# Two chains of small steps on one TensorE: filler products between the two steps of a round, or behind both

## The chip, the cores and the metric

The kernel runs on one core of a Trainium2 chip, in one launch. The metric is the device time of that launch in microseconds (us), the median of several runs. A profiled execution of the same program gives the trace; its span is a little shorter than its time, since the start and the end lie outside it.

The engines are named as in the profile: PE is TensorE's matmul, PEld its weight load, DVE is VectorE, ACT ScalarE, POOL GpSimd, SP SyncE, which issues the DMAs. Each runs its own list of instructions in order, and they wait for each other by semaphores.

## The reference

Sequence 1024, width 1024, batch 1, float32. A first block of two layers (convolution and LRU mixer, mLSTM mixer, two SwiGLUs) is followed by one hybrid layer, and only a stage of that layer is touched:

```python
h = rmsnorm(x, norm_gain)
proj = h @ w_in
(...) = jnp.split(proj, IN_OFFSETS, axis=-1)
ys = (
    gated_deltanet(...),           # chunks of 64, a triangular inverse in each
    spatial_gating(...),
    rwkv7_time_mix(...),
    native_sparse_attention(...),  # compressed, selected and window attention
)
gates = jnp.split(jax.nn.sigmoid(merge), N_MIXERS, axis=-1)
mixed = gates[0] * (ys[0] @ w_branch[0])
for i in range(1, N_MIXERS):
    mixed = mixed + gates[i] * (ys[i] @ w_branch[i])
return x + mixed @ w_out
```

`merge` is the last 4096 columns of `proj`. Nothing in the four mixers needs them, they are only needed at the merge.

## The kernel before, in words

Every float32 product is made of three matmuls on split operands: `xhalf` (high and low part) by `whi`, and `xhalf` by `wlo` (L476). A weight block `wraw` of 128x1024 comes by DMA (L315), ScalarE rounds it to `whi` (L325), GpSimd takes `wlo` (L333), and VectorE, ScalarE and SyncE take away the results.

**The stage of the scans** is the part from 2802 to 3612 us of the profile. Three kinds of work stand in it:

- **Stream A**: the gated deltanet, then the preparations of the sparse attention. Written as a Python generator for each engine; between two `yield`s stands one *step*. A step on PE is a handful of matmuls, and the next step of the stream needs what VectorE and ScalarE made of them.
- **Stream B**: the spatial gating of the two halves, three empty steps (`wait_steps(RWKV_LATER)`), then the RWKV recurrence in chunks.
- **Gates**: the 512 products of `h` with the merge columns (2 halves x 32 tiles x 8 products). A *gate step* is one such product on PE. On the other engines the same step count moves on the rest of it: the split of the next weight block (L325 on ACT, L333 on POOL), and after every eighth product the scaling (L2775 on DVE), the tanh (L2792 on ACT) and the store `g_keep` and the next `wraw` load on SP (L2815, L315). They depend on neither stream and are there to fill PE.

**What sets the order** is `weave_beside`: it takes one step of A, then one of B, and so on, and counts them both, so that A's steps have the odd numbers and B's the even ones. An A step and the B step after it are called a round here; there are some 167 rounds in the stage. Behind *each* step it takes 1 + `MORE_GATES`[number] gate steps. The same call with the same numbers orders all five engines, so that their lists agree. Below, A313 is step 313, of stream A, and B314 the one after it.

`MORE_GATES` holds most extra products behind A steps: 12 behind A1, 5 behind A47, A111 and A115, 7 behind A251, 6 behind A313; and 7 and 8 behind B226 and B228. SyncE has a table of its own, `LOADS_AHEAD`, which differs only in steps 1 and 4.

Where the steps stand in the code: A1 is the matmuls L2941 of `rows`, B2 those of `sg` (L2941 too, in the spatial gating), A3 is L2875. In B, L3592 to L3610 are the two kinds of step of the RWKV chunks late in the stage, and L3719 and L3725 are what VectorE makes of them. In A, L3989 belongs to the compressed attention and needs what L4039 to L4042 make on VectorE.

The attention after the scans uses the same function for its own streams.

Of the kernel before, what the change touches and what calls it, by code (L numbers as in the profile page):

```python
# [870 lines left out]
def wait_steps(n):  # L871
    for _ in range(n):
        yield
# [1105 lines left out]
def rounds(*streams):  # L1979

    live = list(streams)
    while live:
        for s in list(live):
            if next(s, StopIteration) is StopIteration:
                live.remove(s)
        yield
# [1431 lines left out]
def spatial_tensor(pe, K, Q, H, B, j):  # L3418
    n, mm = ("sg", j), pe.e.matmul
    spread_tensor(pe, K, Q, (n, "mean"), H.heads, B.V[:, j, :], (n, "in"), halves=2)  # L3420
    yield from wait_steps(3)
    sums_tensor(pe, K, Q, H, (n, "rs"), B.sq[:, j, :])
    yield from wait_steps(3)
    back_tensor(pe, K, Q, (n, "rs"), B.sq[:, j, :], 2)
    yield from wait_steps(3)
    turn_tensor(pe, K, Q, (n, "vt"), B.V[:, j, :], (n, "normed"), halves=2)
    yield from wait_steps(2)
    pe.wait_ge(*K.at("causal sg"))
    for q in range(2):
        b = take(pe, K, Q, n, "mix", q)  # L3430
        pe.wait_ge(*K.at((n, "vt"), "rows"))
        bias = H.sg_b[0:4, :].unsqueeze(1).to_broadcast([4, 4, 128])
        mm(K.ps[:, b, :], H.pair[0:4, j, :], bias, start=True, stop=False, skip_group_check=True)
        for s in range(2):
            p = part(s, 64)
            for i in range(4):
                d = mm(K.ps[p, b, part(i)], B.VT[:, j, 4 * q + i, p], H.sg_w[:, 2 * j + s, :], start=False, stop=True, skip_group_check=True)
        d.then_inc(*K.T((n, "mix", q)))
    yield
    yield  # L3440


def spatial_vector(ve, K, H, B, j):
    n, V = ("sg", j), K.V
    x, rs, u = B.V[:, j, :], B.rs[:, j, :], B.U[:, j, :]
    yield
    for h in range(2):
        ve.wait_ge(*K.at((n, "mean"), "mm", h))
        ve.own().scalar_tensor_tensor(out=x[:, HALVES[h]], in0=K.bank((n, "mean"), h), scalar=-1.0 / 64, in1=x[:, HALVES[h]], op0=MUL, op1=ADD).then_inc(*V((n, "centred"), ("free", ((n, "mean"), h))))
    yield from wait_steps(3)  # L3450
    sums_vector(ve, K, (n, "rs"), B.rows[j], 1e-5)
    yield
    back_vector(ve, K, (n, "rs"), B.rows[j], B.sq[:, j, :])
    yield from wait_steps(3)
    ve.wait_ge(*K.at((n, "rs"), "rs"))
    ve.own().tensor_tensor(x, x, rs, MUL).then_inc(*V())
    ve.own().tensor_scalar(x, x, K.vec("sg_ln_gain", j), K.vec("sg_ln_bias", j), MUL, ADD).then_inc(*V((n, "normed")))
    yield
    ve.own().tensor_tensor(u, u, B.Z[:, j, :], MUL).then_inc(*V())
    yield from wait_steps(3)  # L3460
    for q in range(2):
        ve.wait_ge(*K.at(n, "mix", q))
        ve.own().tensor_tensor(u[:, HALVES[q]], u[:, HALVES[q]], K.bank(n, "mix", q), MUL).then_inc(*V((n, "y"), ("free", (n, "mix", q))))
    yield


def spatial_scalar(se, K, H, B, j):
    n = ("sg", j)
    yield from wait_steps(2)
    square_scalar(se, K, (n, "rs"), B.V[:, j, :], B.sq[:, j, :], (n, "centred"))  # L3470
    yield from wait_steps(5)
    back_scalar(se, K, (n, "rs"), B.rs[:, j, :], 2)
    yield from wait_steps(3)
    turn_scalar(se, K, (n, "vt"), B.VT[:, j, :, :], halves=2)
    yield from wait_steps(3)


def spatial_gpsimd(ge, K, H, B, j):
    yield from wait_steps(4)
    sums_gpsimd(ge, K, (("sg", j), "rs"), B.rows[j])  # L3480
    yield from wait_steps(SPATIAL_STEPS - 4)
# [8 lines left out]
def spatials(stream):  # L3490

    return rounds(stream(0), in_turn(wait_steps(1), stream(1)))
# [806 lines left out]
LOADS_AHEAD = {**MORE_GATES, 1: 0, 4: 12}  # L4299


def weave_beside(gates, *streams, more={}):

    live, steps = list(streams), 0
    while live:
        for s in list(live):
            if next(s, StopIteration) is StopIteration:
                live.remove(s)
            steps += 1
            for _ in range(1 + more.get(steps, 0)):  # L4310
                next(gates, None)


RWKV_LATER = 3
# [26 lines left out]
def in_turn(*streams):  # L4341
    for s in streams:
        yield from s


def scans_tensor(pe, K, R):
    H, g, s, w = R.H, R.gdn, R.sg, R.rw
    QA, QB = K.QA, K.QB
    pe.wait_ge(*K.at("hybrid constants"))
    gates = gates_tensor(pe, K, H.N)  # L4350
    weave_beside(gates, in_turn(gdn_tensor(pe, K, QA, H, g), nsa_tensor(pe, K, QA, H, R.nsa)),
                 in_turn(spatials(lambda j: spatial_tensor(pe, K, QB, H, s, j)), wait_steps(RWKV_LATER), rwkv_tensor(pe, K, QB, H, w)), more=MORE_GATES)
    pe.reach("scanned")

    def first():
        given_up(pe, K, QA, QB)
        chosen_tensor(pe, K, R.nsa)

    attend_streams(gates, staggered(lambda kind, h: attend_tensor(pe, K, R.nsa, kind, h, K.QC)), wait_steps(ATTEND_STEPS), first=first)


def scans_vector(ve, K, R):
    H, g, s, w = R.H, R.gdn, R.sg, R.rw
    gates = gates_vector(ve, K, H.N, R)
    weave_beside(gates, in_turn(gdn_vector(ve, K, H, g), nsa_vector(ve, K, H, R.nsa)),
                 in_turn(spatials(lambda j: spatial_vector(ve, K, H, s, j)), wait_steps(RWKV_LATER), rwkv_vector(ve, K, H, w)), more=MORE_GATES)
    ve.reach("scanned")

    def first():
        ve.after(K, "scanned")  # L4370
        chosen_vector(ve, K, R.nsa)

    attend_streams(gates, staggered(lambda kind, h: attend_vector(ve, K, H, R.nsa, kind, h)), wait_steps(ATTEND_STEPS), first=first)
    ve.mine.mark(("attended",))


def scans_scalar(se, K, R):
    H, g, s, w = R.H, R.gdn, R.sg, R.rw
    gates = gates_scalar(se, K, H.N, R)
    weave_beside(gates, in_turn(gdn_scalar(se, K, H, g), nsa_scalar(se, K, H, R.nsa)),  # L4380
                 in_turn(spatials(lambda j: spatial_scalar(se, K, H, s, j)), wait_steps(RWKV_LATER), rwkv_scalar(se, K, H, w)), more=MORE_GATES)
    se.reach("scanned")
    attend_streams(gates, staggered(lambda kind, h: attend_scalar(se, K, R.nsa, kind, h)),
                   in_turn(at_steps(*(lambda i=i: results_back_scalar(se, K, R, i) for i in range(2))), wait_steps(ATTEND_STEPS - 16)), first=lambda: se.after(K, "scanned"))


def scans_gpsimd(ge, K, R):
    H, g, s, w = R.H, R.gdn, R.sg, R.rw
    gates = gates_gpsimd(ge, K)
    weave_beside(gates, in_turn(gdn_gpsimd(ge, K, H, g), wait_steps(NSA_STEPS)),  # L4390
                 in_turn(spatials(lambda j: spatial_gpsimd(ge, K, H, s, j)), wait_steps(RWKV_LATER), rwkv_gpsimd(ge, K, H, w)), more=MORE_GATES)
    ge.reach("scanned")
    attend_streams(gates, staggered(lambda kind, h: wait_steps(ATTEND_STEPS)),
                   in_turn(at_steps(*(lambda i=i: results_back_gpsimd(ge, K, R, i) for i in range(2))), wait_steps(ATTEND_STEPS - 16)), first=lambda: ge.after(K, "scanned"))


def scans_sync(sy, K, R, chunk0):
    g, s, w, B = R.gdn, R.sg, R.rw, R.nsa

    def rwkv_first():  # L4400
        yield from wait_steps(12)
        for j in range(2):
            sy.wait_ge(*K.at((("sg", j), "vt"), "turned"))
        rwkv_load(sy, K, w, 0, 0)

    sy.after(K, "hy projected")
    sy.projected(K)
    gates = gates_sync(sy, K, R.H.N, R, chunk0)
    weave_beside(gates, in_turn(gdn_sync(sy, K, g, lambda: nsa_load(sy, K, B)), nsa_sync(sy, K, B)),
                 in_turn(rounds(spatials(lambda j: spatial_sync(sy, K, s, j)), rwkv_first()), wait_steps(RWKV_LATER), rwkv_sync(sy, K, w)), more=LOADS_AHEAD)  # L4410

    def first():
        sy.wait_ge(*K.at("y kept", 1))
        sy.after(K, "scanned")
        attend_load(sy, K, B)
        for i in range(2):
            results_back_sync(sy, K, R, i)

    attend_streams(gates, staggered(lambda kind, h: wait_steps(ATTEND_STEPS)),
                   in_turn(wait_steps(6), at_steps(*(lambda i=i: results_back_sync(sy, K, R, i) for i in range(2, 4))), wait_steps(ATTEND_STEPS - 22)), first=first, lead=8)  # L4420
# [742 lines left out]
```

## Time and profile before

| | us |
|---|---|
| median of 3 runs | 4012.09 |
| lowest, highest | 4011.49, 4012.41 |
| profiled execution: its time | 4012.28 |
| its span | 4010.5 |
| PE busy in the span | 3772.6 |
| DVE, ACT, POOL busy | 2630.1, 1343.8, 1193.1 |
| the scans (2802 to 3612): length, PE busy | 810.0, 766.7 |
| DVE, ACT, POOL busy in them | 413.0, 226.8, 185.6 |

The profiled execution is within 0.2 us of the median, so that sums made on its trace can be laid on the median. A busy PE is not a PE at full speed: PEclk is the share of the full TensorE clock that was granted in a stretch, 1.00 being 2.4 GHz and 0.50 1.2 GHz.

### The profile page before, as it was taken

How to read it: one execution, taken by the hardware profiler on the slowest of the kernel's cores; microseconds unless marked ns; L12 is line 12 of the kernel's file. 1: busy time of each engine (PE TensorE's matmuls, PEld its weight loads, DVE VectorE, ACT ScalarE, POOL GpSimd, SP SyncE). 2: the span in 40 equal slices, each digit the busy share in tenths (PEclk: the TensorE clock that was granted, in tenths of full speed). 3: DMA queues.
4: the chain of work that ended last, by engine and by line, in shares of the span. 5: the costliest groups of instructions: out<-in, count | busy, mean ns of one | idle time of the engine just before them, and what ended most of it. 6: DMA issues, size and time to landing. Idle time of an engine off the chain costs nothing.

```text
span 4010.5 us, 51700 instructions
## 1 busy us (share of the span) xinstructions
PE 3772.6 (94%) x20718; PEld 2957.9 (74%) x20718; DVE 2630.1 (66%) x2926; ACT 1343.8 (34%) x1756; POOL 1193.1 (30%) x578
## 2 busy tenths in 40 slices
PE   8999899999889999999999998999999989998998
PEld 7567788877666666778887776887777767776777
DVE  6964887789874554378788988741455454547783
ACT  5243432234333333243223434211333232324522
POOL 2012144444313333214444441222222212222064
PEclk9999999999989999999999998999999989999999
DMA  3002233345320010222324532323312222323063
GB/s 114 21 21 89 100 101 107 108 154 183 120 80 32 32 37 22 90 105 89 108 93 166 181 121 96 109 91 107 125 59 69 82 72 72 118 89 95 34 209 142
DMA packets 131768, 385.57 MB, mean 96 GB/s; under 512 B 13564, under 2 KB 14208, under 8 KB 126280
## 3 DMA queue, kind: packets, MB, share of 16 engines
q1 hardware_dynamic: 131528, 382.27, 27.5%
q8 instruction: 163, 2.67, 0.3%
q14 instruction: 77, 0.63, 0.0%
HBM read 281.00 MB, written 101.22 MB: 95 GB/s over the span
## 4 chain that ended last, share of the span: by engine, by line
PE 71%; DVE 22%; ACT 4%; issue 1%; POOL 1%; DMA 1%; DVEq 0%; SPq 0%; ACTq 0%; POOLq 0%
PE ps L380 22%; PE ps L1453 21%; PE ps L476 9%; PE ps L4476 2%; PE ps L907 2%; PE ps L2250 1%; PE ps L2971 1%; DVE top L1626 1%; DVE acc L1722 1%; PE ps L2242 1%; DVE xop L1626 1%; PE ps L3064 1%; DVE x L661 1%; PE ps L2988 1%; DVE t L641 1%
## 5 line engine op out<-in xcount | busy, mean ns | idle before, releaser
L333 POOL TENSOR_TENSOR wlo<-wraw,whi 128x1024 fp32r<-128x1024 f32 x181 | 447.8, 2474 | 1712.1 <-ACT whi L325 1703.7
L1453 PE MATMUL ps<-xop,whi 128*128 128x512 f32 x1984 | 617.7, 393 | 14.7 <-DVE acc L1747 9.8
L325 ACT ACTIVATE whi<-wraw 128x1024 fp32r<-128x1024 f32 x185 | 196.1, 1060 | 887.6 <-PE ps L380 605.4
L1453 PE MATMUL ps<-top,whi 128*128 128x512 f32 x1488 | 470.7, 398 | 19.7 <-DVE acc L1716 15.9
L1453 PEld LDWEIGHTS ps<-xop,whi 128*128 128x128 f32 x1984 | 373.0, 188 | 99.7 <-DVE acc L1747 12.3
L1453 PE MATMUL ps<-xop,wlo 128*128 128x512 f32 x992 | 388.2, 391 | 0.0
L476 PE MATMUL ps<-xhalf,whi 128*128 128x512 f32 x1024 | 369.7, 443 | 0.2 <-POOL wlo L333 0.2
L1453 PEld LDWEIGHTS ps<-top,whi 128*128 128x128 f32 x1488 | 282.3, 190 | 88.3 <-DVE acc L1716 19.1
L1851 POOL TENSOR_TENSOR wlo<-wsum,whi 128x1024 fp32r<-128x1024 f32 (+2 forms) x102 | 228.9, 2244 | 363.5 <-ACT whi L1478 363.0
L380 PE MATMUL ps<-xhi,whi 128*128 128x512 f32 x868 | 306.7, 435 | 18.8 <-DVE xlo L681 6.7
L1453 PE MATMUL ps<-top,wlo 128*128 128x512 f32 x744 | 294.7, 396 | 0.0
L380 PE MATMUL ps<-xhalf,whi 128*128 128x512 f32 x1012 | 273.9, 393 | 11.0 <-DVE xhalf L681 8.6
L380 PE MATMUL ps<-xlo,whi 128*128 128x512 f32 x868 | 273.0, 396 | 0.0
L380 PE MATMUL ps<-xhi,wlo 128*128 128x512 f32 x868 | 271.7, 395 | 0.0
L1851 POOL TENSOR_TENSOR wlo<-wraw,whi 128x1024 fp32r<-128x1024 f32 (+2 forms) x80 | 182.6, 2283 | 245.5 <-ACT whi L1478 243.6
L380 PEld LDWEIGHTS ps<-xhalf,whi 128*128 128x128 f32 x1012 | 191.0, 189 | 53.5 <-DVE xhalf L681 11.2
L476 PEld LDWEIGHTS ps<-xhalf,whi 128*128 128x128 f32 x1024 | 178.0, 198 | 53.4 <-issue 23.7
L1453 PEld LDWEIGHTS ps<-xop,wlo 128*128 128x128 f32 x992 | 186.7, 188 | 41.0
L380 PEld LDWEIGHTS ps<-xhi,whi 128*128 128x128 f32 x868 | 161.0, 193 | 74.5 <-issue 27.4
L476 PE MATMUL ps<-xhalf,wlo 128*128 128x512 f32 x512 | 209.1, 408 | 0.0
L1478 ACT ACTIVATE whi<-wsum 128x1024 fp32r<-128x1024 f32 (+2 forms) x108 | 101.9, 943 | 299.9 <-PE ps L1453 126.7
L380 PEld LDWEIGHTS ps<-xlo,whi 128*128 128x128 f32 x868 | 165.9, 191 | 36.8
(641 smaller groups left out, 7091.4 us busy)
## 6 DMA issues: line engine op xcount, KB each, us to landing
wraw<-in_w_dram SPq DMA_DIRECT2D x185, 512.0 KB, 3.6
h_keep<-h SPq DMA_DIRECT2D x154, 256.0 KB, 4.5
wraw<-in_s_dram SPq DMA_DIRECT2D x48, 512.0 KB, 4.1
f<-h_keep SPq DMA_DIRECT2D x24, 768.0 KB, 5.4
wmore<-in_s_dram SPq DMA_DIRECT2D x32, 512.0 KB, 4.0
x_keep<-x SPq DMA_DIRECT2D x16, 1024.0 KB, 3.8
g_keep<-gates SPq DMA_DIRECT2D x64, 256.0 KB, 2.4
gb<-g_keep SPq DMA_DIRECT2D x32, 512.0 KB, 4.1
```

The costliest lines, as they stand in the source:

```text
L325: se.own().activation(K.hi(c), K.raw[:, c % NRAW, :], ACT.Copy).then_inc(*K.S(("hi", c)))
L333: ge.own().tensor_tensor(K.lo(c), K.raw[:, c % NRAW, :], K.hi(c).bitcast(F32), SUB).then_inc(*K.G(("lo", c)))
L380: done = pe.e.matmul(into[:, h, :], wt, x[h], start=(first and j == 0), stop=(last and j == 2), skip_group_check=True)
L476: done = mm(K.ps[:, b, :], wt, x, start=(i == 0 and j == 0), stop=(i == n - 1 and j == 2), skip_group_check=True)
L641: ve.own().tensor_tensor(acc, acc, sq, ADD).then_inc(*K.V((n, "add", i), (n, "add")))
L661: ve.own().tensor_tensor(X[:, i, :], X[:, i, :], Y.out[:, i, :], ADD).then_inc(*K.V((n, "x", i)))
L907: d = mm(K.ps[:, banks[h], :], M.diag[:, (BY_PE.index(j) * P_TAPS + k) % NDIAG, :], M.Yc[:, j, 512 * h + k:512 * h + k + 512], start=(k == ...
L1453: d = pe.e.matmul(out[:, s, :], w[:, o], x[:, i, :], start=(j < 3 and i == 0 and t == 0), stop=(i == k - 1 and t == 2), skip_group_check=True)
L1478: se.own().activation(F.whi(c), F.source(b, j), ACT.Copy).then_inc(*K.S((n, "whi", c)))
L1626: ve.own().tensor_tensor(F.olo[j][:, :k, :], source[:, :k, :], F.ohi[j][:, :k, :].bitcast(F32), SUB).then_inc(*K.V((F.name, "op", g, j)))
L1851: seat.own().tensor_tensor(F.wlo(c), F.source(b, j), F.whi(c).bitcast(F32), SUB).then_inc(*signal((F.name, "wlo", c)))
L4476: done = mm(into, w, x, start=(i == 0 and j == 0), stop=(i == 7 and j == 2), skip_group_check=True)
```

## The change

`weave_beside` gets an argument `behind`. Without it, gate steps follow each step as before. With `behind=-1`, the gate steps that are due are only counted, and are taken behind the step of the last stream that is still live, that is behind B's. So a round was A, its gates, B, its gates; it is A, B, and the gates of both. When one stream has ended, the other is the last one, and gates follow each of its steps. All five calls in the scans get `behind=-1`; the attention's call doesn't.

```diff
-def weave_beside(gates, *streams, more={}):
-
-    live, steps = list(streams), 0
+def weave_beside(gates, *streams, more={}, behind=None):
+
+    live, steps, due = list(streams), 0, 0
     while live:
         for s in list(live):
             if next(s, StopIteration) is StopIteration:
                 live.remove(s)
             steps += 1
-            for _ in range(1 + more.get(steps, 0)):
-                next(gates, None)
+            due += 1 + more.get(steps, 0)
+            if behind is None or not live or s is live[behind]:
+                for _ in range(due):
+                    next(gates, None)
+                due = 0
...
-                 in_turn(spatials(lambda j: spatial_tensor(pe, K, QB, H, s, j)), wait_steps(RWKV_LATER), rwkv_tensor(pe, K, QB, H, w)), more=MORE_GATES)
+                 in_turn(spatials(lambda j: spatial_tensor(pe, K, QB, H, s, j)), wait_steps(RWKV_LATER), rwkv_tensor(pe, K, QB, H, w)), more=MORE_GATES, behind=-1)
```

PE, start of the stage. `rows` are A1's operands, `sg` B2's, `xhalf` by `whi` and `wlo` is a gate product (a pair of rows), and L2875 is A3; 13 such pairs are taken away and put back in the two gaps:

```order
 L2941 MATMUL ps<-rows,c_175 128x512 x2
-L476 MATMUL ps<-xhalf,whi 128x512 x2
-L476 MATMUL ps<-xhalf,wlo 128x512
...
 L2941 MATMUL ps<-sg,c_175 128x512 x2
 L476 MATMUL ps<-xhalf,whi 128x512 x2
 L476 MATMUL ps<-xhalf,wlo 128x512
+L476 MATMUL ps<-xhalf,whi 128x512 x2
+L476 MATMUL ps<-xhalf,wlo 128x512
...
 L2875 MATMUL ps<-c_175,g 128x2 x8
```

The 13 products that stood between A1 and B2 stand behind B2 now, 14 in a row before A3.

PE, late in the stage, around A313 (the first L3989) and B314 (L3606, L3610); again 7 pairs go and come in the gaps:

```order
 L3989 MATMUL ps<-const,n 128x128 x4
-L476 MATMUL ps<-xhalf,whi 128x512 x2
-L476 MATMUL ps<-xhalf,wlo 128x512
...
 L3606 MATMUL ps<-r 128x128
 L3610 MATMUL ps<-r 64x128 x2
 L476 MATMUL ps<-xhalf,whi 128x512 x2
 L476 MATMUL ps<-xhalf,wlo 128x512
+L476 MATMUL ps<-xhalf,whi 128x512 x2
+L476 MATMUL ps<-xhalf,wlo 128x512
...
 L3989 MATMUL ps<-const,n 128x128 x4
```

The seven products between A313 and B314 are behind B314. VectorE's rows at this place do not change up to L3719.

ACT, around B42. L3761 and L2915 make the operands of B42 on PE (L2875 of `r`), L2792 is the tanh of a finished gate tile, L325 a weight split:

```order
 L325 ACTIVATE whi<-wraw 128x1024
-L2792 ACTIVATE gates<-ps 128x512
 L3761 ACT_TABLE_LOAD
 L3761 ACTIVATE r<-ps,vec 128x512 x2
 L2915 ACTIVATE r<-r 128x512
-L325 ACTIVATE whi<-wraw 128x1024
+L2792 ACTIVATE gates<-ps 128x512
 L3768 ACT_TABLE_LOAD
```

The tanh of the gate tile now stands behind stream B's three operations instead of ahead of them. PE has the same rows in both kernels, 9217 when equal neighbours are taken together, in another order.

## Rows read from the trace of the kernel before

**Rows 1.** Page, part 1: busy time, share of span and instructions by engine.

```profile
PE 3772.6 (94%) x20718; PEld 2957.9 (74%) x20718; DVE 2630.1 (66%) x2926; ACT 1343.8 (34%) x1756; POOL 1193.1 (30%) x578
```

**Rows 2.** Windows: length, busy of PE, PEld, DVE, ACT, POOL; PEclk, DMA share, GB/s.

```profile
2802.00:3612.00 810.00, 766.74 (x7674) 594.65 (x7675) 412.96 (x692) 226.76 (x340) 185.57 (x79) 0.93 0.26 87
...
3240.00:3305.00 65.00, 52.78 (x263) 38.94 (x264) 37.91 (x62) 21.87 (x36) 8.58 (x4) 0.76 0.18 61
...
3095.74:3100.00 4.26, 4.26 (x15) 3.52 (x17) 2.19 (x4) 0.00 (x0) 0.00 (x0) 0.50 0.01 3
...
2903.00:2910.00 7.00, 6.71 (x85) 5.47 (x86) 3.67 (x10) 0.24 (x1) 0.00 (x0) 0.76 0.23 90
```

**Rows 3.** Waits of PE, 2802 to 3612: total us, times, longest.

```profile
PE ps L3064 <- DVE r L3679: 9.2, 3, 4.1
...
PE ps L2875 <- ACT r L2915: 3.6, 2, 2.1
```

**Rows 4.** Timeline of PE, stage start: start, us, line, count, idle before.

```profile
2802.19 2.08 PE L2941 MATMUL ps<-rows,c 4*128 4x512 f32 x4 [3.84 <-POOL wlo L333]
2804.20 1.22 PE L476 MATMUL ps<-xhalf,whi 128*128 128x512 f32 x2
...
2808.20 0.84 PE L476 MATMUL ps<-xhalf,whi 128*128 128x512 f32 x2
...
2815.27 1.88 PE L2941 MATMUL ps<-sg,c 128*128 128x512 f32 x4
...
2817.68 1.51 PE L2875 MATMUL ps<-c,g 128*128 128x2 f32 x13
```

**Rows 5.** Tile `sg`, 2800 to 2819: its loads, and their time to landing.

```profile
L2860 SPq DMA_DIRECT2D sg<-p_keep x6: 432/452/707, 2805.7 to 2808.6; - x6
...
DMA to landing us min/median/max: 5.7/7.6/9.1
```

**Rows 6.** Timeline of PE around A313 and B314.

```profile
3551.15 0.66 PE L3989 MATMUL ps<-const,n 128*128 128x128 f32 x4 [0.93 <-DVE n L4042]
...
3556.67 0.49 PE L3606 MATMUL ps<-r 128*128 128x128 f32 x2
...
3558.26 0.60 PE L3989 MATMUL ps<-const,n 128*128 128x128 f32 x4
```

**Rows 7.** Timeline of DVE at the same place.

```profile
3546.37 0.59 DVE L3725 SCALAR_TENSOR_TENSOR r<-r,ps 64x64 f32<-64x64 f32 x2 [2.34 <-PE ps L3606]
3547.07 1.22 DVE L4039 TENSOR_REDUCE n<-n 128x16 f32<-128x1024 f32 x1
...
3556.32 0.29 DVE L3719 SCALAR_TENSOR_TENSOR r<-ps,r 128x128 f32<-128x128 f32 x1
```

**Rows 8.** Timeline of ACT ahead of B42.

```profile
2895.92 1.06 ACT L325 ACTIVATE whi<-wraw 128x1024 fp32r<-128x1024 f32 x1 [6.91 <-PE ps L476]
2899.17 0.60 ACT L2792 ACTIVATE gates<-ps 128x512 f32<-128x512 f32 x1 [2.19 <-DVE ps L2775]
2899.87 1.28 ACT L3761 ACT_TABLE_LOAD   x1
...
2902.61 0.63 ACT L2915 ACTIVATE r<-r 128x512 f32<-128x512 f32 x1
```

**Rows 9.** Timeline of PE after B124's wait.

```profile
3095.74 2.08 PE L3064 MATMUL ps<-r 64*128 64x128 f32 x8 [4.09 <-DVE r L3679]
```

**Rows 10.** Timeline of PE, switches between products and small steps.

```profile
3180.73 0.73 PE L476 MATMUL ps<-xhalf,whi 128*128 128x512 f32 x2
...
3182.32 1.15 PE L2971 MATMUL ps<-inv 64*64 64x64 f32 x32
...
3188.20 0.73 PE L476 MATMUL ps<-xhalf,whi 128*128 128x512 f32 x2
...
3189.09 0.27 PE L2988 MATMUL ps<-inv 64*64 64x64 f32 x1
```

**Rows 11.** Weight loads (PEld) by line, 2802 to 3612.

```profile
L2988 PEld LDWEIGHTS ps<-inv 64*64 64x64 f32 x1280 | 44.3, 144 | 15.8 <-issue 12.8 <-DVE ps L2775 1.4 <-DVE r L3644 0.4
```

More of the change, by code:

```diff
@@ L4365, in scans_vector @@
     weave_beside(gates, in_turn(gdn_vector(ve, K, H, g), nsa_vector(ve, K, H, R.nsa)),
-                 in_turn(spatials(lambda j: spatial_vector(ve, K, H, s, j)), wait_steps(RWKV_LATER), rwkv_vector(ve, K, H, w)), more=MORE_GATES)
+                 in_turn(spatials(lambda j: spatial_vector(ve, K, H, s, j)), wait_steps(RWKV_LATER), rwkv_vector(ve, K, H, w)), more=MORE_GATES, behind=-1)
     ve.reach("scanned")
@@ L4380, in scans_scalar @@
     weave_beside(gates, in_turn(gdn_scalar(se, K, H, g), nsa_scalar(se, K, H, R.nsa)),
-                 in_turn(spatials(lambda j: spatial_scalar(se, K, H, s, j)), wait_steps(RWKV_LATER), rwkv_scalar(se, K, H, w)), more=MORE_GATES)
+                 in_turn(spatials(lambda j: spatial_scalar(se, K, H, s, j)), wait_steps(RWKV_LATER), rwkv_scalar(se, K, H, w)), more=MORE_GATES, behind=-1)
     se.reach("scanned")
@@ L4390, in scans_gpsimd @@
     weave_beside(gates, in_turn(gdn_gpsimd(ge, K, H, g), wait_steps(NSA_STEPS)),
-                 in_turn(spatials(lambda j: spatial_gpsimd(ge, K, H, s, j)), wait_steps(RWKV_LATER), rwkv_gpsimd(ge, K, H, w)), more=MORE_GATES)
+                 in_turn(spatials(lambda j: spatial_gpsimd(ge, K, H, s, j)), wait_steps(RWKV_LATER), rwkv_gpsimd(ge, K, H, w)), more=MORE_GATES, behind=-1)
     ge.reach("scanned")
@@ L4409, in scans_sync @@
     weave_beside(gates, in_turn(gdn_sync(sy, K, g, lambda: nsa_load(sy, K, B)), nsa_sync(sy, K, B)),
-                 in_turn(rounds(spatials(lambda j: spatial_sync(sy, K, s, j)), rwkv_first()), wait_steps(RWKV_LATER), rwkv_sync(sy, K, w)), more=LOADS_AHEAD)
+                 in_turn(rounds(spatials(lambda j: spatial_sync(sy, K, s, j)), rwkv_first()), wait_steps(RWKV_LATER), rwkv_sync(sy, K, w)), more=LOADS_AHEAD, behind=-1)
     def first():
```

## The prediction, made before the changed kernel ran

> **What bounds the kernel now.** I read the page first: PE is busy for 94% of the span, the next engine, DVE, for 66% [rows 1]. Then the windows, for the stage of the scans alone, since all that moves stands in it. PE is busy for 766.7 of 810 us there, DVE for 413.0; 43.3 us of PE are idle, and the mean granted clock is 0.93 [rows 2]. The clock stands at full or half, so 0.93 means that about (1 - 0.93) x 810 / 0.5 = 113 us of the stage ran at 1.2 GHz. The stage is bound by PE's list of work in most places, and by the chains of the two streams in some: from 3240 to 3305 PE is busy for only 52.8 of 65 us and its clock is 0.76 [rows 2]. The waits of PE name those places: the longest sum, 9.2 us in three waits, is of B steps for DVE, another 3.6 us in two for an ACT row of stream B [rows 3]. No wait for gate operands is of weight. The work itself stays as it is, so there are four things to price: places where the gate products were cover for a transfer or another engine and no longer are, places where stream B gets its operands sooner, the cost of switching PE between products and small steps, and the clock.
>
> **The rule for cover.** Between A(k) and A(k+1) PE still has the gates and the B step, and between B(k) and B(k+1) the gates and the A step. What a step can hide before its own stream's next step is nearly unchanged; only the extra products behind an A step now lie one step later for B. A stream B step loses if its operands become ready late in those products. So I compared, for each B step, when its operands were ready with when PE came to it. At the large blocks behind A47, A111, A115, A179, A251 and A303 the operands had been ready for longer than the moved products take, or the B step is empty. Two places are left, A1 and A313.
>
> **Start of the stage: +9.** A1 runs at 2802.19, thirteen products begin at 2804.20, and B2 begins at 2815.27, A3 at 2817.68 [rows 4]. B2 needs `sg`, six loads of 512 KB issued from 2805.7 to 2808.6, which land in up to 9.1 us [rows 5]. That puts the first load, which B2 waits for, between 2811.4 and 2814.8; the trace's event for it is at 2813.9, so that PE had 1.35 us to spare. With the change B2 stands directly behind A1, so PE has nothing to do from 2804.2 to 2813.9, 9.7 us. Then come B2, 2815.27 to the next product at 2816.59 = 1.32 us, and fourteen products. Ten products from 2808.20 to B2 at 2815.27 are 7.07 us, 0.71 each with the switch at their end, 0.69 without. A3 then begins at 2813.9 + 1.3 + 14 x 0.69 = 2824.9, 7.2 us late. That is the low end of this edit. The high end adds the clock. At 2804.20 the engine came from 3.84 us of idle time, and its first three products took (2808.20 - 2804.20) / 3 = 1.33 us each; after B124's wait of 4.09 us a row of eight matmuls lasts 2.08 us, and the window behind it has a granted clock of 0.50 [rows 2, 4, 9]. If B2 and three products run so, 1.3 + 3 x 0.64 = 3.2 us come on top: +10.4. I take +9, nearer to the high end, since both such waits of the trace were followed by the half clock. A later wait of stream B could swallow some of it; this puts the low end at +5.
>
> The Trainium skill, page "TensorE: Matmul & The Clock Gate", section "HAM oscillation — how this bites in real kernels", speaks against the change here: idle gaps between bursts of matmuls send the array back to 1.2 GHz, and the next burst pays. Rows 9 agree with it, with 2.08 us at clock 0.50. By it both new gaps would be at their high ends; without it both at the low ones.
>
> **A313 and B314: +5.** A313 begins at 3551.15 and gives way at 3551.56 to seven products; B314 begins at 3556.67 and A315 at 3558.26 [rows 6]. B314 waits for L3719, and on DVE eight operations of the attention (L4039 to L4042, twice) stand from 3547.07 ahead of it; L3719 runs from 3556.32 to 3556.61 [rows 7]. So seven products, 3551.56 to 3556.6, hid DVE work. The order of DVE does not change there, so B314 stays at 3556.67, or 0.7 us sooner at best, as L3725 at 3546.37 may come one product earlier. PE idles for 5.1 us, and then has B314 (0.78 us, to the next product) and eight products: 3556.67 + 0.78 + 8 x 0.69 = 3562.97 for A315, against 3558.26: +4.7. Low end with the 0.7 us: +4.0; high end with B314 and four products at half clock, + 0.4 + 4 x 0.6: +7.5. I take +5.
>
> **B42: -2.** B42 waited for ACT's L2915, for 2.1 of the 3.6 us in rows 3. L2915 at 2902.61 stands behind L3761's table load at 2899.87, and this behind a gate's tanh at 2899.17, for which ACT had been idle for 2.19 us [rows 8]. The tanh moves behind L2915. L3761 can then begin after L325, from 2897.0 if its operand is there, which it must be by 2899.87. L2915 ends up to 2.9 us sooner; PE's wait of 2.1 us can go in full but no more. So between 0 and -2.1, and another -1.7 if the half-clock stretch behind this wait goes too: from 2903 to 2910 the clock is 0.76 [rows 2], and (1 - 0.76) x 7 = 1.7. I take -2.
>
> **Switches: -9.** Two products in a row between 64-row steps take 3182.32 - 3180.73 = 1.59 us, one alone 3189.09 - 3188.20 = 0.89 us, while one inside a run takes 0.70 [rows 10]. The difference of 0.19 is lost before the 64x64 weight load; the loads of L2988 alone sat idle for 12.8 us with "issue" as their only reason [rows 11]. The change merges the two places of products in a round into one, so it saves one such switch, if PE is not waiting for operands anyway. Of the rounds, 119 have matmuls in both steps, and in 24 of these PE waits at B. Where both steps are 64-row ones (some 18 rounds) I count 0.3 us, since the switch into the products costs some 0.1 as well: 5.4. In the 77 others, with 128-row steps on one side, a product takes 0.79 or less before the step, and I count 0.05: 3.6. Together -9. The ends: nothing but the 64-row rounds at 0.19, -4; and 0.19 in all 95, -18.
>
> The same page, section "Back-to-back issue gap", would give less: it has loads and matmuls pipelined, with spacing set by both, so that the order of unlike ones should not matter. Rows 10 show a gap that it does not tell of. By it this term is 0, and the sum +12.
>
> **Everything else: 0.** Gate work of ACT, DVE, POOL and SP moves behind B's rows by one step. That makes B's rows earlier and the gates' tiles free later by about 0.7 us; the weight split has blocks in hand, and no wait of rows 3 names it. In the stretches bound by chains, as 3240 to 3305, the chain is the same and the products only change sides. I take 0, between -2 and +4. SP's `g_keep` stores and weight loads also move behind B's loads, which are few.
>
> **The sum.** 9 + 5 - 2 - 9 + 0 = +3. On the profiled execution's 4012.28 this is 4015.3, on the median, 0.19 lower, 4015.1. Low ends together: 5 + 4 - 3.8 - 18 - 2 = -15; high ends: 10.4 + 7.5 + 0 - 4 + 4 = +18.
>
> **The rivals.**
> *Slower: the clock (4027).* One mechanism: PE's half-clock stretches follow idle time, and grouping makes idle time longer in one piece and products denser in another. Both gaps at their high ends, the switches worth only 4, and up to six further half-clock stretches at 1.7 us each, as after B42's wait: 10.4 + 7.5 - 2 - 4 + 10.2 = +22 at most, and +15 with two of them. It decides once the waits of a round fall together in the chain-bound stretches. For it: 113 us already run at half clock. Against: the total of idle time hardly changes apart from the two gaps.
> *Slower: cover lost one product at a time (4025).* PE comes to some 28 B steps within 0.1 us of their operands. If each moved forward by a product and found nothing, 28 x 0.69 = 19 us would be exposed, which with the +3 of the sum is +22; with half of them it is +12.7. Against: those operands come from the B step before, which moves forward as well. It decides only where B's operands come from A's DVE work, as at A313.
> *Faster: switches (4002).* Gaps at their low ends, 5 + 4, B42 -3.8, switches -15: -10. For it: "issue" stands behind a great part of PEld's idle time. Against: much of that is hidden behind the matmul before.
> *The change does nothing (4012).* If B2's operand were there at 2804, or DVE's block were reordered. Rows 5 and 7 exclude both.
>
> **How the numbers follow.** The forecast, two new gaps paid mostly by fewer switches: 0.58. Clock: 0.14. Lost cover: 0.13. Switches win: 0.13. Nothing: 0.02. A measurement tells 0.2%, 8 us, from no change. The forecast's own range is 4006 to 4023, so 0.05 of its 0.58 is beyond +8. Faster by over 8 us: 0.11 (most of its rival). Slower by over 8: 0.05 + 0.14 + 0.11 = 0.30. Within: 0.59. The range with 8 in 10 is 4003 to 4027.
>
> **What would show it.** On PE's timeline: idle time of 9 to 10 us behind A1, a `sg` step at half clock, and A3 some 9 us late; at A313 an idle stretch of 4 to 5 us that ends at L3719. L2915 ahead of L2792 on ACT and no wait at B42. Idle time of PEld by "issue" lower by about 9 us in the stage. PE's idle time in the scans up from 43 to about 56 us, while PE's busy time is up by the clock or down by the switches. Wrong would be: `sg` landing before A1 ends, a wait for L476's operands in the long runs, or new waits of B steps outside the two places.

## The result, and the profile after

The changed kernel takes 4035.6 us (median of 4 runs, 4034.1 to 4047.7) beside 4012.25 for the kernel before (median of 4, 4011.5 to 4021.0): 1.0052 times, 95% interval 1.0037 to 1.0068, or 15 to 27 us more. That is outside the predicted range of 4003 to 4027.

The profiled execution took 4034.1 us, span 4032.3. Inside the scans, from A1's first matmul to the end of the last step of stream B, it was 814.0 us beside 795.0 before, +18.9. The other 2.9 us of the two spans lie in stretches whose instructions are the same in both kernels, 1.5 of them ahead of A1.

Windows of the changed kernel, the scans from A1 to B334, then the first 4.0 us from B2 on and 3.6 us from B314 on; columns as in [rows 2]:

```profile
2803.68:3617.65 813.97, 743.44 (x7616) 588.54 (x7617) 414.74 (x686) 222.85 (x335) 179.98 (x77) 0.93 0.25 83
...
2816.90:2820.90 4.00, 3.97 (x6) 1.87 (x7) 0.00 (x0) 0.00 (x0) 0.00 (x0) 0.54 0.50 204
...
3571.40:3575.00 3.60, 3.57 (x11) 2.62 (x12) 1.95 (x4) 0.88 (x2) 0.00 (x0) 0.51 0.02 5
```

The same stretch of the kernel before:

```profile
2802.19:3597.22 795.03, 751.96 (x7616) 582.57 (x7617) 408.94 (x686) 222.84 (x335) 180.73 (x77) 0.93 0.25 86
```

PE is busy for 8.5 us *less* and idle for 70.5 us instead of 43.1. So PE's own work did become cheaper, and the loss is 27.5 us of new idle time. Not all of the 8.5 us belongs to the order, though. The kernel in which all engines but PE have the changed order was profiled twice (see the experiments). The two windows of its scans differ by 7.9 us of PE's busy time:

```profile
2805.14:3594.67 789.53, 748.93 (x7616) 581.03 (x7617) 407.85 (x686) 222.86 (x335) 179.88 (x77) 0.94 0.26 86
...
2801.73:3597.76 796.03, 756.80 (x7616) 587.12 (x7617) 408.80 (x686) 222.96 (x335) 179.13 (x77) 0.93 0.26 85
```

The first has 92.0 us of PE's busy time at half clock, the second 108.5. A matmul takes about twice as long at half clock (a product 1.28 us instead of 0.69, below), so busy time less half of its half-clock part is PE's work as if at full clock. In the scans that is 702.6 to 703.9 us in the ten traces in which PE's order is that of before or differs in one or two rounds, and 696.3 to 696.7 us in the four with all of its rounds, or all but two, joined; the three kernels with a part of the rounds joined lie between. So the order is worth 6.7 us of work, and the other 1.8 of the 8.5 are half-clock time that differs between the two traces (97.9 and 94.3 us).

The waits of PE, to be read beside [rows 3]; first two more of the kernel before:

```profile
PE ps L2941 <- DVE r L3669: 5.4, 4, 2.6
...
PE ps L3559 <- ACT r L2932: 3.0, 1, 3.0
```

and then those of the changed kernel:

```profile
PE ps L2941 <- DMA sg<-p_keep: 11.2, 1, 11.2
PE ps L3064 <- DVE r L3679: 8.9, 3, 4.1
PE ps L2941 <- DVE r L3669: 8.4, 4, 3.3
PE ps L3606 <- DVE r L3719: 5.5, 1, 5.5
PE ps L3559 <- ACT r L2932: 4.3, 2, 3.7
...
PE ps L2875 <- ACT r L2915: 2.7, 3, 2.1
...
PE ps L2988 <- DVE inv L3026: 2.2, 1, 2.2
```

The first and the fourth row are new and are the two places of the prediction, 16.7 us together. The rest, 10.8 us of new idle time, is spread over small waits of both streams: L3669's is up by 3.0 us, L2932's by 1.3, and L3026's, 2.2 us, is new. 5.9 of the 10.8 us lie in steps 189 to 229, from 3247 to 3369 us of the trace before, the stretch that the prediction called bound by chains.

The start of the stage on PE's timeline, for [rows 4]:

```profile
2803.68 2.08 PE L2941 MATMUL ps<-rows,c 4*128 4x512 f32 x4 [3.86 <-POOL wlo L333]
...
2816.93 3.78 PE L2941 MATMUL ps<-sg,c 128*128 128x512 f32 x4 [11.17 <-DMA sg<-p_keep]
2819.72 1.44 PE L476 MATMUL ps<-xhalf,whi 128*128 128x512 f32 x2
...
2821.24 0.62 PE L476 MATMUL ps<-xhalf,whi 128*128 128x512 f32 x2
...
2830.11 1.84 PE L2875 MATMUL ps<-c,g 128*128 128x2 f32 x16
```

From A1 to A3 are 26.43 us, 15.49 before: +10.9. B2 took 2.79 us to the next product instead of 1.32, at a granted clock of 0.54, and the first product 1.52 instead of 0.69. In return the three slow products behind A1 [rows 4] are gone: between A1 and A3 PE is busy at half clock for 5.7 us, 6.5 before. So here the slow work has only moved, and the +10.9 is the wait of 11.2 us. A313 and B314, for [rows 6]:

```profile
3565.24 0.66 PE L3989 MATMUL ps<-const,n 128*128 128x128 f32 x4 [0.23 <-DVE n L4042]
...
3571.43 0.79 PE L3606 MATMUL ps<-r 128*128 128x128 f32 x2 [5.54 <-DVE r L3719]
...
3572.78 1.22 PE L476 MATMUL ps<-xhalf,whi 128*128 128x512 f32 x2
...
3579.38 0.60 PE L3989 MATMUL ps<-const,n 128*128 128x128 f32 x4
```

From A313 to A315 are 14.14 us, 7.11 before: +7.0. The wait is 5.5 us of it, and B314 and the products behind it cost some 1.7 us more than at full clock. VectorE's rows are the ones of [rows 7], in the same order. On ACT, the table load for B42 stands ahead of the tanh, for [rows 8]:

```profile
2908.51 1.28 ACT L3761 ACT_TABLE_LOAD   x1
2909.81 1.41 ACT L3761 ACTIVATE r<-ps,vec 128x512 f32<-128x512 f32 x2
2911.31 0.63 ACT L2915 ACTIVATE r<-r 128x512 f32<-128x512 f32 x1
2912.05 0.60 ACT L2792 ACTIVATE gates<-ps 128x512 f32<-128x512 f32 x1
```

The weight loads have less idle time by "issue": those of L2988, for [rows 11], have half of it left, those of the products 13.9 of 23.2 us. First the kernel before, then the changed one:

```profile
L476 PEld LDWEIGHTS ps<-xhalf,whi 128*128 128x128 f32 x926 | 161.5, 199 | 50.3 <-issue 23.2 <-ACT gates L2792 0.2 <-POOL wlo L333 0.2
...
L476 PEld LDWEIGHTS ps<-xhalf,whi 128*128 128x128 f32 x928 | 173.1, 200 | 48.0 <-issue 13.9
L2988 PEld LDWEIGHTS ps<-inv 64*64 64x64 f32 x1280 | 43.3, 141 | 13.2 <-issue 6.4 <-DVE inv L3026 3.0 <-DVE ps L2775 2.2
```

These two rows alone are down by 15.7 us, where the prediction had looked for 9 in the whole stage, and PE's work fell by 6.7: most of a load's idle time had been hidden behind the matmul before it.

### The profile page after: what moved, and what is told of

Same layout as the page of the kernel before. It is cut to its first block, busy times and chain, and to the rows that moved or that the text cites. A ratio compares the mean times of both kernels' runs of the same rounds, so it can differ in the third digit from the quotient of the medians.

```text
span 4032.3 us, 51693 instructions
## 1 busy us (share of the span) xinstructions
PE 3766.4 (93%) x20718; PEld 2964.3 (74%) x20718; DVE 2639.7 (65%) x2926; ACT 1343.9 (33%) x1756; POOL 1195.5 (30%) x578
## 3 DMA queue, kind: packets, MB, share of 16 engines
q1 hardware_dynamic: 131528, 382.27, 27.5%
## 4 chain that ended last, share of the span: by engine, by line
PE 68%; DVE 24%; ACT 4%; issue 2%; POOL 1%; DMA 1%; DVEq 0%; SPq 0%; ACTq 0%; POOLq 0%
PE ps L380 22%; PE ps L1453 21%; PE ps L476 8%; PE ps L4479 2%; PE ps L907 2%; PE ps L2250 1%; DVE top L1626 1%; DVE acc L1722 1%; PE ps L2242 1%; DVE xop L1626 1%; PE ps L2971 1%; DVE x L661 1%; PE ps L3064 1%; PE ps L2988 1%; DVE t L641 1%
## 5 line engine op out<-in xcount | busy, mean ns | idle before, releaser
L325 ACT ACTIVATE whi<-wraw 128x1024 fp32r<-128x1024 f32 x185 | 196.1, 1060 | 933.2 <-PE ps L380 607.8
L1453 PE MATMUL ps<-top,whi 128*128 128x512 f32 x1488 | 471.6, 398 | 19.4 <-DVE acc L1716 16.0
L1453 PEld LDWEIGHTS ps<-xop,whi 128*128 128x128 f32 x1984 | 373.4, 189 | 99.4 <-DVE acc L1747 11.7
L476 PE MATMUL ps<-xhalf,whi 128*128 128x512 f32 x1024 | 358.3, 432 | 0.3 <-POOL wlo L333 0.3
L380 PE MATMUL ps<-xhalf,whi 128*128 128x512 f32 x1012 | 275.0, 394 | 10.4 <-DVE xhalf L681 7.9
L380 PEld LDWEIGHTS ps<-xhalf,whi 128*128 128x128 f32 x1012 | 191.7, 190 | 52.4 <-DVE xhalf L681 9.8
L476 PEld LDWEIGHTS ps<-xhalf,whi 128*128 128x128 f32 x1024 | 189.2, 199 | 51.0 <-issue 14.5
```

The lines of the kernel that those rows point to most:

```text
L325: se.own().activation(K.hi(c), K.raw[:, c % NRAW, :], ACT.Copy).then_inc(*K.S(("hi", c)))
L380: done = pe.e.matmul(into[:, h, :], wt, x[h], start=(first and j == 0), stop=(last and j == 2), skip_group_check=True)
L476: done = mm(K.ps[:, b, :], wt, x, start=(i == 0 and j == 0), stop=(i == n - 1 and j == 2), skip_group_check=True)
L1453: d = pe.e.matmul(out[:, s, :], w[:, o], x[:, i, :], start=(j < 3 and i == 0 and t == 0), stop=(i == k - 1 and t == 2), skip_group_check=True)
```

## A way to read two traces of reordered work

PE's matmuls other than the products (19182 of them) have the same order in both kernels. So the n-th of them in one trace is the n-th in the other, and the difference of their starts, less the one at A1, is how far the changed kernel has fallen behind at that step. Read at A steps it is +10.9 at A3, 9.9 at A41, 7.2 at A43, 5.7 at A47, 3.2 at A85, 6.2 at A91 to A121, 11.5 at A131, 9.5 at A141, 10.4 at A155 to A195, 7.0 at A209, 10.5 at A227, 9.7 to A255, 11.8 at A257, 12.6 at A313, 19.6 at A315 and 19.4 at A329. Two steps of +10.9 and +7.0 stand out. Between them it wanders from 2.1 (A81) to 13.3 (A295) and comes back to within 1.7 us of where it began. Whether the wandering means anything was a question for the chip.

A part of it comes from the trace of before, which is one execution too: in the nine other traces with PE's order as before but for a round or two, the distance to it falls by 3.1 us from A131 to A147, because that one trace has 13.7 us at half clock from A131 to A155 where they have 3.4.

## The experiments

Theory 1: two waits that lost their cover make up the loss. Theory 2: it is spread over many small waits and half-clock stretches. In the kernels that join rounds by number, `weave_beside` got one more condition, and `joined(step)` says after which steps the gate products may wait:

```diff
-            if behind is None or not live or s is live[behind]:
+            if behind is None or not live or s is live[behind] or not joined(steps):
```

Differences are to the kernel before, by the ratio of the runs and its interval, times 4014 us; "in the scans" is the difference between the traces in the length from A1 to the end of B334. Three of the kernels below ran only once and are read only at the place in question: the half cover, and rounds 41 and 39 alone.

**Only the first round joined:** `return step == 1`.

> Only the first round is joined (B2 directly behind A1, the 14 gate products behind B2); all other steps keep their order of before. Theory 1 (two waits that lost their cover make up nearly all of the loss, 10.9 us at A3 and 7.0 us at A315): +10 to +11 us on the kernel before, 4022 to 4023, with PE idle for some 11 us ahead of B2 and about 4 us at half clock behind it, and no other difference of over 1 us. Theory 2 (the loss is the sum of many small waits and of half-clock stretches that fall elsewhere; the place itself is partly taken back later by waits of stream B that it swallows): +3 to +7.

Measured: +0.37% (0.24 to 0.50), +15 us (10 to 20). In the scans +12.8, of which +12.0 at A3. Its timeline of PE:

```profile
2809.37 2.08 PE L2941 MATMUL ps<-rows,c 4*128 4x512 f32 x4 [3.82 <-POOL wlo L333]
2822.55 3.78 PE L2941 MATMUL ps<-sg,c 128*128 128x512 f32 x4 [11.10 <-DMA sg<-p_keep]
2836.85 0.39 PE L2875 MATMUL ps<-c,g 128*128 128x2 f32 x3
```

The wait and the half-clock B2 are there with this round alone, and none of it is given back later. The 12.0 us at A3 are 1 us above what theory 1 had expected, the +15 of the runs more, with +10 to +11 just inside their interval.

**Only the round of A313 and B314 joined:** `return step == 313`.

> Only the round of A313 and B314 is joined. Theory 1: +6 to +7 us on the kernel before, 4018 to 4019, PE idle for 5 us ahead of B314 and at half clock behind. Theory 2: +2 to +4, the rest of the 7 us seen in the changed kernel having come from work that was late already.

Measured: +0.25% (0.15 to 0.36), +10 us (6 to 14). In its trace A313 to A315 takes 14.76 us instead of 7.11, +7.7:

```profile
3549.75 0.66 PE L3989 MATMUL ps<-const,n 128*128 128x128 f32 x4 [0.94 <-DVE n L4042]
...
3555.24 0.80 PE L3606 MATMUL ps<-r 128*128 128x128 f32 x2 [4.83 <-DVE r L3719]
...
3560.60 1.06 PE L476 MATMUL ps<-xhalf,whi 128*128 128x512 f32 x2
...
3564.51 0.60 PE L3989 MATMUL ps<-const,n 128*128 128x128 f32 x4
```

The wait is 4.8 us, and the fourth product at 3560.60 still lasts 1.06 us a pair where one at full clock lasts 0.62: four products at half clock, 1.28 us each, against one to two in the changed kernel. So theory 1 has its second place, 0.7 us dearer in the trace than its upper end of 7.

**Both places left as before, all other rounds joined:** `return step not in (1, 313)`.

> The changed kernel with A1 and A313 followed by their own gate products again, as before; all other rounds are joined. Theory 1: the 17.9 us of the two places go, 4034.1 - 17.9 = 4016, that is +2 to +5 on the kernel before, since the new small waits (about 11 us more idle time of PE outside the two places) stand against the 9 us of PE time saved by fewer switches. Theory 2: the gain is under 12 us and the time stays at or over 4022.

Measured: -0.09% (-0.20 to +0.02), -4 us (-8 to +1). In the scans +3.1. With the two places taken out the loss is gone, and 15 + 10 us of the two alone are, within their intervals, the 21 us of the whole. Theory 2 is excluded, and theory 1 holds, though the time lies a little under its range of +2 to +5. But the window shows that the rest is not the gain of 11 us that the prediction had added up for it:

```profile
2803.97:3602.06 798.09, 743.57 (x7616) 588.97 (x7617) 413.45 (x686) 222.73 (x335) 179.45 (x77) 0.93 0.25 85
```

PE is busy for 8.4 us less than before (6.6 of them work, the rest less half-clock time) and idle for 54.5 us, 11.5 more.

**Half of the cover at each place,** with the order of before:

```diff
-MORE_GATES = {1: 12, 18: 3, ... 303: 2, 313: 6}
+MORE_GATES = {1: 6, 2: 6, 18: 3, ... 303: 2, 313: 3, 314: 3}
-LOADS_AHEAD = {**MORE_GATES, 1: 0, 4: 12}
+LOADS_AHEAD = {**MORE_GATES, 1: 0, 2: 0, 4: 12}
```

> The order of before, but the extra products of the two places are shared: 7 products behind A1 and 7 behind B2 (13 and 1 before), 4 behind A313 and 4 behind B314 (7 and 1 before). It is read at the two places on the trace. If the loss is the missing cover alone, six products fewer ahead of B2 make PE wait for 2 to 4 us and A3 comes 3 to 4 us later against A1 than before; at A315 1.5 to 2.5 us later, with an idle stretch of about 2 us. If half-clock work after the wait is a part of the price at any length of wait, 1.5 to 2.5 us come on top at each; if it needs the long wait, the granted clock stays at 1.00 behind both waits.

Measured: A3 5.9 us later, A315 2.1 us later. PE's timeline:

```profile
2816.70 3.64 PE L2941 MATMUL ps<-sg,c 128*128 128x512 f32 x4 [4.08 <-DMA sg<-p_keep]
2819.50 1.31 PE L476 MATMUL ps<-xhalf,whi 128*128 128x512 f32 x2
...
3564.66 0.49 PE L3606 MATMUL ps<-r 128*128 128x128 f32 x2 [2.12 <-DVE r L3719]
...
3565.45 0.73 PE L476 MATMUL ps<-xhalf,whi 128*128 128x512 f32 x2
```

Six products fewer, 4.1 us, made 4.1 us of wait, and the matmuls after it ran at half clock, 1.8 us more. Three fewer at the other place, 2.1 us, made 2.1 us of wait and no half-clock work: B314 and the product behind it last what they last before. So half-clock work came on top behind the wait of 4.1 us and not behind the one of 2.1. The cost of missing cover is its length, plus what half-clock work follows.

**Only the stretches where the distance fell / stayed / rose.** `joined` is true for steps 41 to 81, 131 to 147 and 203 to 213; for 91 to 121, 157 to 187 and 229 to 255; and for 123 to 129, 149 to 153, 195 to 201, 217 to 221, 225 to 227, 257 and 295.

> Only the rounds of steps 41 to 81, 131 to 147 and 203 to 213 are joined: the stretches in which the changed kernel came nearer to the one before (at A steps, by 7.8, 2.1 and 6.0 us). If those gains belong to the places, -10 to -16 us on the kernel before. If they are a matter of where the half-clock stretches happen to fall, -2 to -6, with the fall at 203 to 213, where no wait changed, missing.

> Only the rounds of steps 91 to 121, 157 to 187 and 229 to 255 are joined, 46 rounds in stretches bound by PE with 64x64 steps of stream A beside 128-row steps of B. In the changed kernel A's steps kept their distance to the kernel before within 0.3 us through each. Theory: one switch less saves nothing there, -1 to +1. The rival, the prediction's term of switches: 0.05 to 0.19 us a round, -2.5 to -9.

> Only the rounds of steps 123 to 129, 149 to 153, 195 to 201, 217 to 221, 225 to 227, 257 and 295 are joined: the stretches bound by chains in which the changed kernel fell back, by some 17 us in all. If the new waits are due to the joined order at the place, +8 to +17; if they follow from half-clock stretches that fall elsewhere, 0 to +5.

Measured: -0.03% (-0.17 to +0.11), -0.02% (-0.16 to +0.11), and +0.19% (0.06 to 0.31), +8 us (2 to 12). The first expectation was far off: with the falls alone the time is that of before, within -7 to +4 us, so the 16 us weren't a property of those rounds. The flat stretches are flat: their trace holds its distance to 0.4 us through each. PE's work is 1.0 us less over the three, 0.02 us a round, where the prediction had counted 0.05, and small new waits take that up, most at their ends (A257 comes 2.4 us later against A255 than before). In the rises, the joined order does cost something, at the low end of the range for waits that belong to the place.

The trace of the second of these kernels says why single traces mislead. Ahead of step 91 it has the order of before, instruction for instruction, and yet is 9.7 us behind at A73.

**Which engine's order?** PE alone with `behind=-1`; PE alone, with steps 1 and 313 left as before; all engines but PE.

> Only PE's list is in the changed order; DVE, ACT, POOL and SP keep that of before. Tells whose order makes which part. Theory 1: both places are PE's order alone (B2 waits for a DMA, B314 for DVE rows whose order the change leaves), so the 17.9 us stay, but the gain at B42 (4 us, ACT's order) is missing: 4036 to 4040. Rival: the small new waits come from gate work that DVE and ACT take behind stream B's, and go with it: 4024 to 4030.

> Only PE's list is in the changed order, and A1 and A313 are followed by their own products as before. What is left of the PE-only kernel's +28.5 us without the two places (10.8 + 7). If PE's joined order by itself is worth the 9 us of fewer switches: -9 to 0 on the kernel before. If gate rows that DVE and ACT still take between stream A's and B's make PE wait: +7 to +13 us, as 28.5 - 18 says.

> PE keeps the order of before; DVE, ACT, POOL and SP get the changed one. The PE-only kernel lost 31.4 us within the scans where the full change lost 18.5, so the order of the other engines should be worth some -4 (B42) on this side and its lack the rest on that. Theory: no wait for sg and none at B314, a gain at B42: -2 to -8 on the kernel before. Rival: with PE's products ahead of B's steps, gate tiles wait behind B's rows on DVE and ACT and PE waits for free banks: +2 to +10.

Measured: +0.71% (0.54 to 0.88), +28 us (22 to 35); +0.17% (0.06 to 0.28), +7 us (2 to 11); and -0.14% (-0.24 to -0.03). The two places are PE's order alone: 28 - 7 = 21 us, and the trace of PE alone has both waits, of 10.9 and 5.5 us. What is left of PE's joined order costs 7 us. Its window, in the scans:

```profile
2810.07:3611.29 801.22, 737.60 (x7616) 585.05 (x7617) 412.69 (x686) 222.73 (x335) 178.46 (x77) 0.94 0.25 85
```

PE is busy for 14.4 us less than before (6.3 of them work, 8.1 half-clock time that fell differently) and idle for 63.6 us, 20.6 more. Some of its waits:

```profile
PE ps L2941 <- DVE r L3669: 9.3, 4, 3.5
...
PE ps L2896 <- DVE r L2903: 5.2, 3, 3.8
PE ps L3559 <- ACT r L2932: 4.9, 4, 3.7
...
PE ps L2875 <- DVE r L3651: 2.5, 1, 2.5
```

PE comes to B's steps a product sooner, and the rows on DVE and ACT that make their operands don't. With those rows ahead of the gates' rows as well, as in the kernel with both places left as before and all engines joined, the new idle time is 11.5 us instead of 20.6. The forecast's range for this "everything else" was -2 to +4.

The other half of the change, without PE's, is a gain. Since its interval came near to 0, it ran again:

> The same kernel as e7_rest_only (all engines but PE in the changed order), with more rounds, since its interval came near to no change and it is the fastest candidate: 0.1 to 0.2% faster than before if the gain at B42 and less half-clock work (98.7 against 108.9 us in the trace of e7_rest_only) are its own; within 0.05% if that trace and its times were luck.

Measured: -0.19% (-0.27 to -0.10), 4008.4 us (median of 11) beside 4014.3 (of 23). So this is the fastest of the kernels here, about 8 us under the kernel before; its first series gave -6. Two kernels looked for the engine that makes it: ACT alone, then ACT and DVE.

> Only ACT's list is in the changed order. The kernel in which all engines but PE have it was 0.14% faster (0.03 to 0.24). If that came from ACT's gate rows moving behind stream B's, above all at B42: 0.05 to 0.2% faster here too. If from DVE's or POOL's: no difference. The Trainium skill has no rule on this.

> DVE and ACT in the changed order, PE, POOL and SP in that of before. All engines but PE gave -0.14% and -0.19%, ACT alone +0.07%. If DVE's and ACT's order together make the gain: -0.1 to -0.2%. If POOL's or SP's part (weight splits and loads moved behind stream B's rows) makes it: -0.05 to +0.07%, as ACT alone.

Measured: +0.07% (-0.05 to +0.20), and -0.08% (-0.21 to +0.04). ACT's order alone doesn't do it. With DVE the sign turns, but the interval holds 0 as well as the full gain; which engine makes it stays open in the times. PE's idle time in the scans points to DVE: it is 43.1 us before, 43.6 with ACT alone, 40.5 with DVE and ACT, and 40.6 and 39.2 in the two traces with all engines but PE. That is 2.5 to 3.9 us of the 8; PE's work is the same in all of them to 1 us, so where the rest comes from isn't shown. (DVE's rows were not tried without ACT's.)

**B42.** Only round 41 joined, then only round 39.

> Only the round of steps 41 and 42 is joined. Read at the place: on ACT L3761's table load ahead of the gate tile's tanh, PE's wait of 2.1 us at B42 gone, and A43 to A45 without half-clock work, so that A45 comes 2.7 to 4 us sooner against A41 than before. Rival (the operand of L3761 is late itself): under 1 us.

> Only the round of steps 39 and 40 is joined, on all engines. The kernel with round 41 joined left the tanh ahead of L3761 on ACT, because ACT's rows for B42 stand in step 40 and the tanh in the gate steps of 39. Read at the place: with round 39 joined the table load comes before the tanh, PE's wait of 2.1 us at B42 goes, and A45 comes 3.5 to 4.5 us sooner against A41. If that needs the order of other rounds too: under 1 us.

Round 41 missed: ACT kept the tanh ahead of the table load, and PE, coming one product sooner, waited 3.0 us instead of 2.1. ACT's rows for B42 stand in step 40, and the tanh in the gate steps behind A39. With round 39 joined, ACT's timeline is that of the changed kernel:

```profile
2905.34 1.06 ACT L325 ACTIVATE whi<-wraw 128x1024 fp32r<-128x1024 f32 x1 [6.90 <-PE ps L476]
2906.49 1.28 ACT L3761 ACT_TABLE_LOAD   x1
...
2909.29 0.63 ACT L2915 ACTIVATE r<-r 128x512 f32<-128x512 f32 x1
2910.03 0.60 ACT L2792 ACTIVATE gates<-ps 128x512 f32<-128x512 f32 x1
```

PE's wait is gone and A45 comes 3.9 us sooner against A41: 2.3 from the wait and 1.6 from half-clock work behind it. With ACT's order alone it is 3.9 as well.

## Why the prediction was wrong, point by point

- **Start of the stage, +9:** right in place and mechanism, +10.9 measured (12.0 and 10.5 in the kernels that have it alone or on PE alone). The mis-sized term was the arrival of `sg`. B2 starts behind the third of its six loads, not the first as the prediction says: wherever it waits, it starts within 0.05 us of that landing. The third load landed 13.2 us after A1, not 11.7 as I took it from the trace of before. In the sixteen other traces it came between 11.9 and 13.4, in the middle of them 12.8, so the one I had was the earliest, and the spare time before B2 is more often 0.3 us than 1.35. With 13.2 the prediction's own sum gives 8.7 without the clock term; the half clock added 2.2 us to that, not the 3.2 of its high end. Nothing of it was swallowed by later waits.
- **A313 and B314, +5:** +7.0 (7.7 alone). The wait of 5.1 us was right (5.5 and 4.8 measured). What failed was to take the low side for the clock here and the high side at the start: both waits are long ones, and half-clock work, 1.7 us here and 3.0 with this round alone, came each time.
- **B42, -2:** the wait went and the half-clock stretch behind it too: A45 comes 3.6 us sooner against A41 in the changed kernel, 3.9 with round 39 alone. The lower end was the value.
- **Switches, -9:** PE's work fell by 6.7 us, so the term was of the right kind and a quarter too large. (Its parts are 5.4 and 77 x 0.05 = 3.9, not 3.6, and its low end 18 x 0.19 = 3.4, not 4; neither changes the outcome.) The flat stretches, 46 of the rounds, gave 1.0 us of the 6.7.
- **Everything else, 0 (-2 to +4):** the step that failed in its reasoning. I argued that B's operands come from the B step before, which moves forward as well, and that chain-bound stretches stay as they are. But the rows on DVE and ACT behind a step don't take less time because PE comes sooner. In the kernel without the two places PE's idle time is up by 11.5 us, the wait of B42 already deducted, against the 6.6 us of work that the order saves. The rival "cover lost one product at a time" had 19 us as its most; some 60% of it came. "New waits of B steps outside the two places" was one of my own signs of being wrong. The idle time is not all a loss: from step 189 to 229 it is up by 5.9 us in the changed kernel, but the half-clock work there is down from 38.0 to 26.8 us, and the stretch takes 122.3 us instead of 122.6.
- **The sum:** in the changed kernel's trace it is 11.2 and 5.5 us of wait at the two places, 10.8 of other new idle time and 8.5 less of busy time, +19.0, or the +18.9 seen in the scans but for rounding. Against the forecast, the two places came to +17.9 instead of +14, and the rest to +1 instead of -11. The runs put the weights differently, within their intervals: 21 to 25 us for the two places (28 - 7, and 21 + 4 with all engines), and -4 (-8 to +1) for the rest. Either way, both parts were too low by several us, and their errors added up.
- **The rivals and the range:** of the rival "the clock", the part that came true is both gaps at their high ends, 10.4 + 7.5 = 17.9. Its further half-clock stretches didn't come: PE's half-clock work in the scans is 94.3 us, 97.9 before. The lost cover came beside it. I had the two as one or the other, gave 0.30 to slower and put the range's end at what either gives alone. This split is read from one trace; the times don't give it.

By the Trainium skill's section "HAM oscillation — how this bites in real kernels" ("TensorE: Matmul & The Clock Gate") both gaps were to be paid at their high ends. The traces agree, with clocks of 0.54 and 0.51 behind waits of 11.2 and 5.5 us.

The Trainium skill's "Back-to-back issue gap" on the same page, as I had read it, would have made the switches worth nothing. PE's work, 6.7 us less with the same matmuls, speaks against that reading; the flat stretches, with 0.02 us a round, come near to it.

## What to carry to other kernels

Filler between two steps is cover for whatever the second one waits for. Before fillers are moved, measure at each place how long the operand of the step behind them had been ready, and do so in more than one execution, since here it was 1.35 us in one trace and about 0.3 in the middle of all. A place with 1.35 us to spare can give one product, not thirteen. The size of a block of fillers doesn't say whether it is cover: of the large ones behind A steps, those of 12 and 6 extra products (A1, A313) were, and those of 5, 5, 5, 4 and 7 (A47, A111, A115, A179, A251) were moved at a cost of at most 0.2 us each. And an order shared by several engines can be tried on each part by itself: here the half that moves evictions behind the chains' rows is a small gain, and the half that moves the products is the loss.

## What the runs showed of the hardware

- In all 17 traces, the granted clock was at half, or fell to it within 1 us, behind every wait of PE of 3.8 us or more in the scans. Behind the one of 2.1 us at B314 it wasn't, behind the one of 2.1 us at B42 it was in part (0.76 over 7 us) [rows 2, 3]: the length of a short wait doesn't decide it. One and the same wait can do either. The wait for L3633 is 2.8 us in the kernel before and 2.7 in the one with only the first round joined, and the instructions around it are the same. The eight matmuls behind it take 1.16 us in the one and 2.07 in the other:

```profile
2939.44 1.16 PE L3064 MATMUL ps<-r 64*128 64x128 f32 x8 [2.84 <-DVE inv L3633]
...
2958.87 2.07 PE L3064 MATMUL ps<-r 64*128 64x128 f32 x8 [2.74 <-DVE inv L3633]
```

- Half-clock stretches fall differently in executions of the same instructions, and in the two traces of one kernel shown with the result that is all of the difference: PE's work is 702.9 and 702.6 us, its idle time 40.6 and 39.2, and half of 92.0 and of 108.5 us are 8.2 us apart, for lengths 6.5 us apart. It also happens where PE doesn't wait. Round 39's and round 41's kernels are the same up to step 39. The first row is of the one, the second of the other, each the 25 us that begin 26.0 us after A1:

```profile
2831.60:2856.60 25.00, 25.00 (x93) 18.74 (x94) 14.23 (x22) 7.98 (x12) 10.27 (x5) 0.59 0.19 63
```

```profile
2832.20:2857.20 25.00, 25.00 (x127) 19.63 (x127) 17.38 (x26) 9.82 (x14) 12.02 (x6) 0.86 0.19 64
```

  PE is busy without a pause in both, and does 93 matmuls in the one and 127 in the other, at clocks of 0.59 and 0.86. One such stretch is some 6 us of the kernel's time.
- The kernel before ran between 4006.2 and 4030.1 us in the later series, with medians of 4014.3 to 4016.2, where its first three runs lay within 1 us of each other at 4012. Three runs said less about its scatter than I took from them, and even with ten to twelve runs of a kernel beside 20 to 30 of the one before, the intervals are 7 to 11 us wide.
